# Two projection units fewer ahead of the first gather, and six units beside the first V products

## The chip, the cores and the metric

The kernel runs on one core of a Trainium2 chip. The metric is the device time of the whole program in microseconds (us). The program drives five engines: TensorE (PE in the profile; PEld is its weight load), VectorE (DVE), ScalarE (ACT), GpSimd (POOL), which here issues the gathers, and SyncE (SP), which issues all other DMAs. The engines run their own instruction streams in program order and meet at semaphores.

## The reference

One layer of a streaming encoder in float32. It is run on a prompt of 1024 rows and on a sample of 32 rows, with the same weights:

```python
h = rmsnorm(x, norm_mix_w);  proj = h @ w_in            # 1024 x 2824
# proj: mLSTM q, k, v, output gate, input and forget gates | attention q, k, v
hm = sigmoid(mo) * head_rmsnorm(mlstm_scan(mq, mk, mv, gates))   # 4 heads of 128
hs = swa(rope(sq), rope(sk), sv, sinks)                          # 8 heads, window 128
x = x + concat(hm, hs) @ w_out
h2 = rmsnorm(x, norm_ffn_w)
# PEER: per row and each of 8 heads, the best 16 of 128 x 128 experts
s1, s2 = keys of both halves of (h2 @ w_q);  idx = best 16 sums of two keys
a = gelu(peer_u[idx] . h2);  x = x + sum(softmax(top) * a * peer_v[idx])
y = rmsnorm(x, norm_final_w)
```

## The kernel before

The rows are cut into nine tiles: tiles 0 to 7 are 128 rows of the prompt, the last is the sample. A tile is projected (`h @ w_in`, in six chunks of 512 columns, the last of 264), mixed (mLSTM and attention, output projection, second norm, queries, key scores), and then goes through the expert stage.

**Expert stage.** A tile's 128 rows go in groups: 32 rows by four heads fill the 128 partitions, and two groups `g` belong to 32 rows. Each group has 16 steps. One step, called a slot `t = 16 g + k`, gathers 128 rows of `peer_u` (for the next group) and 128 rows of `peer_v` (for this group), 0.524 MB each. POOL issues them in turn, U then V, in one queue (`gather_u`, `gather_v`). DVE multiplies U rows by the normalised rows and sums (L1261, a dot); ACT takes the gelu; DVE makes the weights `wk`; PE multiplies them by V rows and adds up in the PSUM tensor `acc` (L1657, a V product). U rows land in a ring of six buffers, V rows in one of seven; a gather waits until its buffer is free. There are 66 groups, 1056 slots, 2112 gathers. The first 16 U gathers, those of group 0, stand at slots -16 to -1.

**Order of the work.** For every engine it is written out. After tile 0, the steps of each later tile's mixing are hung on slots: `slot_of(m, r)` gives the slot of a step with rank `r` of tile `m`; PE_AT, ACT_AT and DVE_AT hold the ranks. On PE rank 5 transposes q and k (`qk_transpose`), 11 to 25 are the mLSTM, 33 to 54 the attention, 58 to 65 the output projection, 75 to 90 the 16 `query` steps, 91 to 94 the key scores. At its slot a step follows the V product on PE and the dot on DVE.

**Before the first gather.** Tile 0 has nothing else to hide behind, so its mixing up to the concatenation is interleaved with other work: projections of tiles 1 to 3, in units. A unit is one chunk of columns for one tile, `(c, m)` in UNITS, and has two halves of four matmuls. There are 18 units for tiles 1 to 3. BEHIND of them are interleaved with tile 0's mixing in `first_tiles`; EARLY_AT says after which half unit which ranks of tile 0 stand. One unit more (number BEHIND) is put between tile 0's output projection and its second transposes. The rest stand on PE at the slots in UNIT_PE, their copies out of PSUM at those in UNIT_ACT (even units) and UNIT_DVE (odd units). All 18 use two halves of `acc` in turn, which is also what V products add into, so the first V product waits until all units are copied (`begin_parts(0)`).

A unit is copied to a buffer (UNIT_PO names it), and SP stores it from there to a scratch tensor in DRAM; tile `m`'s mixing loads it from there (`load_p`). Buffers 5 to 9 are the last three V buffers of the ring, so `gather_v` of the slots 4, 5 and 6 waits until all units that use these buffers are stored. SP also loads the query weights `w_q` in four pieces of 2 MB (`load_wq`) to the place of input weights that no unit needs any more: the first takes the place of chunk 2, the other three those of chunks 3 to 5.

Of the kernel before, what the change touches and what calls it, by code (L numbers as in the profile page):

```python
# [15 lines left out]
DC = D // P  # L16
# [77 lines left out]
EARLY_AT = ((10, 0), (14, 2), (20, 4), (24, 6), (32, 7), (36, 9), (46, 11), (50, 14), (54, 15), (EARLY_END, 16))  # L94


UNITS = [(c, m) for c in range(3) for m in range(1, FIRST)]
BEHIND = len(UNITS)
UNITS += [(3, 1), (4, 1), (5, 1), (3, 2), (3, 3), (4, 2), (4, 3), (5, 2), (5, 3)]
UNIT_PE = {-16: 10, -14: 11, -12: 12, -10: 13, -8: 14, -6: 15, -4: 16, -2: 17}  # L100
UNIT_ACT = {-12: 10, -7: 12, 1: 14, 3: 16}
UNIT_DVE = {-11: 11, -4: 13, 1: 15, 4: 17}

UNIT_PO = [(0, 1, 2, 3, 4, 8)[n % 6] for n in range(BEHIND)] + [4, 5, 6, 7, 8, 9, 4, 5, 6]
# [12 lines left out]
def slot_of(m, r):  # L117

    if m == 1:
        return -4 + r * 85 // 100  # L120
    if m == 2:
        return 78 + r * 120 // 100
    if m == 3:
        return 206 + r * 85 // 100 if r < 51 else 264 + (r - 51) * 88 // 100
    base = AGAIN + PERIOD * NC_ + 1 if m == FIRST else 8 * TOPK * (m - 1)
    points = {FIRST: SLOTS_4, FIRST + 1: SLOTS_5, SAMPLE: SLOTS_SAMPLE}.get(m, SLOTS)
    for (r0, s0), (r1, s1) in zip(points, points[1:]):
        if r <= r1:
            return base + s0 + (r - r0) * (s1 - s0) // (r1 - r0)
# [46 lines left out]
def program(nc, x_prompt, x_sample, cache_k, cache_v, st_c, st_n, st_m, norm_mix_w, w_in, if_bias, mnorm_w, sinks,  # L176
# [15 lines left out]
    with ExitStack() as ctx:  # L192
# [99 lines left out]
        po += [part[:, :]] + [ring[:, NU + 4, 0:512]] + [a[:, h * 512:h * 512 + 512] for a in (ring[:, NU + 5, :], ring[:, NU + 6, :]) for h in range(2)]  # L292
        first = [pj[:, 0:512], pj[:, 512:1024], vx[:, :, 0:MD], pj[:, 1024:1536], pj[:, 1536:2048], pj[:, 2048:PJ]]
# [8 lines left out]
        unit_bank = [acc[:, 0:512], acc[:, 512:1024]]  # L302
# [11 lines left out]
        proj_out = [sem(f"proj_out{b}") for b in range(10)]  # L314
# [43 lines left out]
        def _(sp):  # L358
# [134 lines left out]
            sp.wait_ge(chunk_ready, NC_ + 9)  # L493
            load_wq(0)

# [27 lines left out]
            for b in range(10):  # L523
                sp.wait_ge(proj_out[b], stored(b, len(UNITS)))
# [81 lines left out]
        def _(act):  # L606
# [64 lines left out]
            def unit_copy(n):  # L671
# [5 lines left out]
                S.activation(po[b][:, 0:PC[c][1]], unit_bank[n % 2][:, 0:PC[c][1]], ACT.Copy, scale=nr1[:, m, 2:3])  # L677
# [27 lines left out]
            def mix(s, i, m):  # L705
# [197 lines left out]
        def _(dve):  # L903
# [34 lines left out]
            def unit_copy(n):  # L938
# [4 lines left out]
                V.tensor_scalar(po[b][:, 0:PC[c][1]], unit_bank[n % 2][:, 0:PC[c][1]], nr1[:, m, 2:3], None, ALU.mult)  # L943
# [41 lines left out]
            def mix(s, i, m):  # L985
# [13 lines left out]
                elif s == "qk_copy":  # L999
# [6 lines left out]
                    dve.wait_ge(qk_transposed, m + 1)  # L1006
                    V.tensor_scalar(qkT[:, 4:8, 0:n], mx[:, 3, :].rearrange("p (h t) -> p h t", h=4)[:, :, 0:n], MD ** -0.5, None, ALU.mult)
# [290 lines left out]
        def _(pe):  # L1298
# [315 lines left out]
            def begin_parts(q):  # L1614
# [103 lines left out]
```

## Time and profile before

| | |
|---|---|
| median of 3 runs | 3126.98 us (3126.38 to 3129.21) |
| the profiled execution, its span | 3386.3 us |
| PE busy | 2600.2 us (77%) |
| DVE busy | 2120.6 us (63%) |
| POOL busy | 1995.2 us (59%) |
| ACT busy | 556.3 us (16%) |
| mean DMA rate | 353 GB/s |
| mean granted TensorE clock | 0.811 |

The profiled execution is longer than the timed ones. Its span starts with the first instruction and ends with the last. In a row of the timeline stand the start, the time from start to end, the engine, the line, the operation, what it writes and reads, how many instructions were merged (a float32 matmul is two), and in brackets the idle time of the engine before it and what ended that. "DMA" in the windows is the mean busy share of the 16 DMA engines, "PEclk" the granted TensorE clock as a share of full speed.

### The profile page before, as it was taken

To read this page: it belongs to the slowest core of one execution; us is meant where nothing else is said; L and a number is where in the kernel's file an instruction comes from. 1 tells how busy PE (TensorE), PEld (TensorE's weight loads), DVE (VectorE), ACT (ScalarE), POOL (GpSimd) and SP (SyncE) were. 2 spreads that over 40 slices of the span, in tenths; PEclk is the share of its full clock that TensorE was granted. 3 is DMA by queue.
4 is the path that set the end of the run, shared out by engine and by line. 5 is a ranking of instruction groups with operands and counts; after the bars stand their busy time and mean duration, and the time that the engine had idled before them with its cause. 6 is when DMAs were issued, how large, how long until landed. Compare 5 with 4: busy or idle time off the path is not lost.

```text
span 3386.3 us, 33673 instructions
## 1 busy us (share of the span) xinstructions
PE 2600.2 (77%) x10989; PEld 1007.2 (30%) x10989; DVE 2120.6 (63%) x5282; ACT 556.3 (16%) x1093; POOL 1995.2 (59%) x2128
## 2 busy tenths in 40 slices
PE   8996886678678899987876876678676776686666
PEld 4562351225222533223432331124212331121101
DVE  1256657766676666657667757676667666676653
ACT  2211111211121131122012111111111011111001
POOL 0026556666666566665656666666666666666665
PEclk9997897789677899997987887788667886677667
DMA  6479999999999999999999999999999999999998
GB/s 230 146 275 371 336 338 374 362 371 343 378 351 365 342 400 407 409 382 353 362 329 346 380 354 381 367 364 345 384 360 360 370 365 376 358 368 370 371 363 332
DMA packets 348919, 1197.02 MB, mean 353 GB/s; under 512 B 37760, under 2 KB 54408, under 8 KB 346952
## 3 DMA queue, kind: packets, MB, share of 16 engines
q0 software_dynamic: 304128, 1107.43, 86.7%
q1 hardware_dynamic: 44616, 87.45, 7.0%
q8 instruction: 86, 1.41, 0.2%
q14 instruction: 89, 0.73, 0.1%
HBM read 1180.69 MB, written 14.15 MB: 353 GB/s over the span
## 4 chain that ended last, share of the span: by engine, by line
PE 33%; DVE 16%; issue 13%; POOL 12%; DMA 9%; another core or an unknown queue 8%; DVEq 6%; ACT 1%; ACTq 0%; SPq 0%; POOLq 0%
PE acc L1657 11%; PE mx L1549 7%; DVE ring L1261 7%; POOL ring L593 6%; POOL ring L582 6%; DMA ring<-in_peer_v_dram,idx 5%; DVEq L1148 4%; DMA ring<-in_peer_u_dram,idx 4%; PE mx L1365 3%; PE mx L1531 2%; PE acc L1341 2%; PE mx L1560 2%; PE acc L1328 1%; PE h2p L1603 1%
## 5 line engine op out<-in xcount | busy, mean ns | idle before, releaser
L1657 PE MATMUL acc<-ring,wk 128*32 128x512 f32 x4224 | 1362.6, 742 | 525.6 <-DMA ring<-in_peer_v_dram,idx 289.4
L1261 DVE SCALAR_TENSOR_TENSOR ring<-ring,h2p 128x1024 f32<-128x1024 f32 x1056 | 1273.8, 1215 | 565.4 <-DMA ring<-in_peer_u_dram,idx 315.8
L593 POOL DMA_INDIRECT ring<-in_peer_v_dram,idx x1056 | 997.1, 944 | 707.7 <-issue 269.7
L582 POOL DMA_INDIRECT ring<-in_peer_u_dram,idx x1056 | 996.3, 943 | 667.1 <-issue 292.9
L1657 PEld LDWEIGHTS acc<-ring,wk 128*32 128x32 f32 x4224 | 217.8, 122 | 1406.6 <-issue 670.8
L1549 PE MATMUL mx<-reg,weights 128*128 128x128 f32 x1792 | 256.7, 297 | 40.9 <-issue 38.6
L1549 PEld LDWEIGHTS mx<-reg,weights 128*128 128x128 f32 x1792 | 230.8, 206 | 145.7 <-issue 145.7
L1531 PE MATMUL mx<-weights,reg 128*128 128x512 f32 (+1 forms) x256 | 133.0, 643 | 3.5 <-issue 3.5
L1365 PE MATMUL mx<-weights 128*128 128x512 f32 (+1 forms) x288 | 126.9, 585 | 0.0
L821 ACT ACTIVATE gl<-dots 128x16 f32<-128x16 f32 x66 | 14.2, 216 | 637.5 <-issue 346.1
L1603 PE MATMUL h2p<-ch,ident 32*32 32x512 f32 x528 | 86.7, 708 | 36.6 <-issue 18.9
L1560 PE MATMUL mx<-kT,pj 128*32 128x128 f32 x1040 | 69.4, 313 | 32.9 <-issue 25.3
L781 ACT COPY pj<-mx 128x512 f32<-128x512 f32 x32 | 18.7, 585 | 432.0 <-remote 182.7
L1261 DVE DVE_READ_ACCUMULATOR ring<-ring,h2p 128x1 f32 x1056 | 86.9, 82 | 0.0
L821 ACT ACT_TABLE_LOAD x66 | 84.7, 1283 | 6.5 <-issue 1.1
L815 ACT ACT_TABLE_LOAD x61 | 78.3, 1283 | 19.1 <-issue 11.3
L1365 PEld LDWEIGHTS mx<-weights 128*128 128x128 f32 x288 | 53.4, 195 | 75.8 <-issue 74.3
L1531 PEld LDWEIGHTS mx<-weights,reg 128*128 128x128 f32 (+1 forms) x256 | 44.1, 189 | 96.4 <-issue 96.4
L1560 PEld LDWEIGHTS mx<-kT,pj 128*32 128x32 f32 x1040 | 50.1, 123 | 64.6 <-issue 54.8
L1224 DVE TENSOR_TENSOR xt<-xt,acc 32x1024 f32<-32x1024 f32 x33 | 40.1, 1216 | 45.0 <-PE acc L1612 32.2
L1087 DVE TENSOR_REDUCE s<-mx 128x4 f32<-128x1024 f32 (+1 forms) x18 | 21.0, 1174 | 58.9 <-remote 46.6
L1365 PE MATMUL mx<-weights,reg 128*128 128x512 f32 (+1 forms) x96 | 47.4, 642 | 12.4 <-DMA weights<-in_w_in_dram 6.6
(310 smaller groups left out, 2400.3 us busy)
## 6 DMA issues: line engine op xcount, KB each, us to landing
ring<-in_peer_u_dram,idx POOLq DMA_INDIRECT x1056
ring<-in_peer_v_dram,idx POOLq DMA_INDIRECT x1056
weights<-in_peer_w_q_dram SPq DMA_DIRECT2D x7, 2048.0 KB
weights<-in_w_in_dram SPq DMA_DIRECT2D x5, 2048.0 KB, 18.2
weights<-in_w_in_dram SPq DMA_DIRECT2D x10, 1024.0 KB
ring<-in_peer_w_q_dram SPq DMA_DIRECT2D x8, 1024.0 KB, 5.6
xt<-in_x_prompt_dram SPq DMA_DIRECT2D x8, 512.0 KB
ring<-in_w_out_dram SPq DMA_DIRECT2D x2, 2048.0 KB, 14.2
```

What stands on the lines that cost most here:

```text
L582: pool.indirect_dma_start(ring[:, n % NU, :], None, u_d, bass.IndirectOffsetOnAxis(ap=idx[:, g % 4, k:k + 1], axis=0)).then_inc(u_in[n % N ...
L593: pool.indirect_dma_start(ring[:, NU + n % NV, :], None, v_d, bass.IndirectOffsetOnAxis(ap=idx[:, g % 4, k:k + 1], axis=0)).then_inc(v_in[ ...
L815: S.activation(ew[:, :], top[:, g % 3, :], ACT.Exp, bias=ntop[:, g % 3:g % 3 + 1], accum_out=ez[:, 0:1])
L821: S.activation(gl[:, :], dots[:, g % 2, :], ACT.Gelu)
L1148: dve.drain()
L1261: V.scalar_tensor_tensor(ring[:, n % NU, :], ring[:, n % NU, :], 1.0, h2p[:, :], ALU.mult, ALU.mult, accum_out=dots[:, (g + 1) % 2, k:k + ...
L1365: last = T.matmul(bank, hT1_again[i][:, 4 * half + k, :], wpiece[(2 * p + half) % 3][:, k, 0:w], start=half + k == 0, stop=half == 1 and k ...
L1531: last = T.matmul(mx[0:n, 2 + half, :], t8[:, k, 0:n], w, start=k == 0, stop=k == DC - 1)
L1549: last = T.matmul(mx[:, i // 4, i % 4 * P:i % 4 * P + n], w, t8[:, k, 0:n], start=k == 0, stop=k == DC - 1)
L1560: last = T.matmul(mx[q:q + SUB, i, col:col + NK], qT[:, c, i * SUB:(i + 1) * SUB], kT[:, c % 2, :], start=True, stop=True)
L1603: last = T.matmul(h2p[j * SUB:(j + 1) * SUB, cols], ident[r, r], ch[m % 2][r, cols], start=True, stop=True)
L1657: last = T.matmul(acc[j:j + SUB, cols], wk[:, g % 2, n % TOPK, :], ring[:, NU + n % NV, cols], start=g % 2 == 0 and n % TOPK == 0, stop=g ...
```

## The change

UNITS is cut otherwise: ahead of the first gather now stand seven units and not nine in the interleaved part (both chunks 0 and 1 of the three tiles, and chunk 2 of tile 1), and then one after the output projection as before. Chunk 2 of tiles 2 and 3 goes behind the first gather. EARLY_AT spreads tile 0's steps over 14 half units and not 18.

Of the ten units behind the first gather, four (8 to 11) stand at slots -16 to -7, ahead of the V products. Six (12 to 17, from LATE on) stand at slots 1 to 13 and write to the banks 0 and 1 of the PSUM tensor `mx`, which is otherwise the mixing's. They are copied to four new buffers, 10 to 13, in the SBUF tensor `reg`, also the mixing's. V products wait for the copies of units 0 to 11 only, and slots 4 to 6 of the V gathers for units 8 to 11. Tile 1's mixing begins at slot 16 and not -4 and takes 61 slots per 100 ranks and not 85; it waits for the late units' copies and stores. The first piece of `w_q`, which takes chunk 2's place, is loaded behind unit 11.

```diff
-EARLY_AT = ((10, 0), (14, 2), (20, 4), (24, 6), (32, 7), (36, 9), (46, 11), (50, 14), (54, 15), (EARLY_END, 16))
-UNITS = [(c, m) for c in range(3) for m in range(1, FIRST)]
+EARLY_AT = ((10, 0), (14, 2), (20, 3), (24, 5), (32, 6), (36, 8), (46, 9), (50, 11), (54, 12), (EARLY_END, 13))
+UNITS = [(c, m) for c in range(2) for m in range(1, FIRST)] + [(2, 1)]
 BEHIND = len(UNITS)
-UNITS += [(3, 1), (4, 1), (5, 1), (3, 2), (3, 3), (4, 2), (4, 3), (5, 2), (5, 3)]
-UNIT_PE = {-16: 10, -14: 11, -12: 12, -10: 13, -8: 14, -6: 15, -4: 16, -2: 17}
+UNITS += [(3, 1), (4, 1), (5, 1), (2, 2), (2, 3), (3, 2), (3, 3), (4, 2), (4, 3), (5, 2), (5, 3)]
+LATE = 12
+UNIT_PE = {-16: 8, -13: 9, -10: 10, -7: 11, 1: 12, 3: 13, 6: 14, 8: 15, 11: 16, 13: 17}
...
-UNIT_PO = [(0, 1, 2, 3, 4, 8)[n % 6] for n in range(BEHIND)] + [4, 5, 6, 7, 8, 9, 4, 5, 6]
+UNIT_PO = [(0, 1, 2, 3, 4, 8)[n % 6] for n in range(BEHIND)] + [4, 5, 6, 7, 8] + [10, 11, 12, 13, 10, 11]
...
     if m == 1:
-        return -4 + r * 85 // 100
+        return 16 + r * 61 // 100
...
+        po += [reg[:, 512 * i:512 * i + 512] for i in range(4)]
...
-        unit_bank = [acc[:, 0:512], acc[:, 512:1024]]
+        unit_bank = [acc[:, n % 2 * 512:n % 2 * 512 + 512] if n < LATE else mx[:, n % 2, :] for n in range(len(UNITS))]
...
             for n in range(6, BEHIND):
                 store_unit(n)
-            sp.wait_ge(chunk_ready, NC_ + 9)
-            load_wq(0)
...
                     act.wait_ge(qk_transposed, m + 1)
+                    if m == 1:
+                        for b in range(10, 14):
+                            act.wait_ge(proj_out[b], stored(b, len(UNITS)))
...
                         pe.wait_ge(chunk_dve if n % 2 else chunk_act, 3 + n // 2)
+                        if n == LATE:
+                            pe.wait_ge(sc_ready, 1)
...
+                    elif m == 1:
+                        pe.wait_ge(chunk_act, 3 * FIRST)
+                        pe.wait_ge(chunk_dve, 3 * FIRST)
+                        pe.wait_ge(p_in, p_landed(m))
+                        pe.wait_ge(sc_ready, m)
...
                 elif q == 0:
-                    pe.wait_ge(chunk_act, 3 * FIRST)
-                    pe.wait_ge(chunk_dve, 3 * FIRST)
+                    pe.wait_ge(chunk_act, 3 + LATE // 2)
+                    pe.wait_ge(chunk_dve, 3 + LATE // 2)
```

PE at the first V products, in the kernel before. `mx<-kT,pj` are tile 0's last key scores, `acc<-weights` with `ch1` or `xt1` are units of tiles 2 and 3, `acc<-ring,wk` are V products (two matmuls each), `mx<-ident,pj` is tile 1's first mixing step.

```order
L1560 MATMUL mx<-kT,pj 32x128 x56
L1341 MATMUL acc<-weights 128x512 x8
L1341 MATMUL acc<-weights 128x264 x8
L1341 MATMUL acc<-weights,ch1 128x512 x8
L1341 MATMUL acc<-weights,xt1 128x512 x8
L1341 MATMUL acc<-weights,ch1 128x512 x8
L1341 MATMUL acc<-weights,xt1 128x512 x8
L1341 MATMUL acc<-weights,ch1 128x264 x8
L1341 MATMUL acc<-weights,xt1 128x264 x8
L1436 MATMUL mx<-ident,pj 128x128 x8
L1657 MATMUL acc<-ring,wk 32x512 x12
```

The same place in the changed kernel, where L1348 are units and L1669 V products.

```order
L1572 MATMUL mx<-kT,pj 32x128 x56
L1348 MATMUL acc<-weights 128x512 x8
L1348 MATMUL acc<-weights 128x264 x8
L1348 MATMUL acc<-weights,ch1 128x512 x8
L1348 MATMUL acc<-weights,xt1 128x512 x8
L1348 MATMUL mx<-weights,ch1 128x512 x8
L1669 MATMUL acc<-ring,wk 32x512 x6
L1348 MATMUL mx<-weights,xt1 128x512 x8
L1669 MATMUL acc<-ring,wk 32x512 x6
L1348 MATMUL mx<-weights,ch1 128x512 x8
L1669 MATMUL acc<-ring,wk 32x512 x4
L1348 MATMUL mx<-weights,xt1 128x512 x8
```

Five units stand ahead of the first V product in place of eight, then units and V products alternate.

PE in the query steps of tile 1, in the kernel before. L1549 is one `query` step (eight matmuls), L1657 a V product.

```order
L1549 MATMUL mx<-reg,weights 128x128 x8
L1657 MATMUL acc<-ring,wk 32x512 x2
L1549 MATMUL mx<-reg,weights 128x128 x8
L1657 MATMUL acc<-ring,wk 32x512 x2
L1549 MATMUL mx<-reg,weights 128x128 x8
L1657 MATMUL acc<-ring,wk 32x512 x2
L1549 MATMUL mx<-reg,weights 128x128 x16
```

The same place in the changed kernel.

```order
L1561 MATMUL mx<-reg,weights 128x128 x8
L1669 MATMUL acc<-ring,wk 32x512 x2
L1561 MATMUL mx<-reg,weights 128x128 x16
L1669 MATMUL acc<-ring,wk 32x512 x2
L1561 MATMUL mx<-reg,weights 128x128 x8
L1669 MATMUL acc<-ring,wk 32x512 x2
L1561 MATMUL mx<-reg,weights 128x128 x16
```

From the first to the last of the 16 query steps there were 13 V products, now there are 9.

## Rows read from the trace of the kernel before

**Rows 1.** Window of 20 us ahead of the first gather: span, busy time by engine, PEclk, DMA, GB/s.

```profile
60.00:80.00 20.00, 20.00 (x80) 11.14 (x79) 3.35 (x15) 4.30 (x11) 0.00 (x0) 1.00 0.08 28
```

**Rows 2.** Timeline of POOL: U gathers L582, V gathers L593, from the first on.

```profile
191.99 1.09 POOL L582 DMA_INDIRECT ring<-in_peer_u_dram,idx  x1 [189.34 <-DVEq L1204]
...
230.84 0.94 POOL L593 DMA_INDIRECT ring<-in_peer_v_dram,idx  x1 [0.30 <-issue]
...
259.67 0.94 POOL L593 DMA_INDIRECT ring<-in_peer_v_dram,idx  x1 [19.19 <-DMA proj_scratch<-ring]
...
264.84 0.94 POOL L593 DMA_INDIRECT ring<-in_peer_v_dram,idx  x1 [3.00 <-DMA proj_scratch<-ring]
```

**Rows 3.** Windows of the gather stage, columns as in rows 1 (the number of POOL's gathers in brackets).

```profile
250.00:255.00 5.00, 1.43 (x11) 1.07 (x9) 2.73 (x9) 2.75 (x5) 0.00 (x0) 1.00 1.02 424
255.00:260.00 5.00, 0.00 (x0) 0.00 (x0) 1.59 (x3) 0.00 (x0) 0.33 (x1) 0.53 0.47 187
260.00:265.00 5.00, 3.85 (x10) 1.06 (x12) 3.66 (x11) 0.00 (x0) 1.70 (x3) 0.50 0.75 237
305.00:477.00 172.00, 139.10 (x561) 60.40 (x561) 120.02 (x300) 28.19 (x62) 104.27 (x111) 0.81 0.93 344
3200.00:3300.00 100.00, 64.54 (x158) 7.29 (x158) 56.49 (x119) 6.94 (x11) 66.70 (x71) 0.62 0.97 366
```

**Rows 4.** Timeline of PE, tile 0's mixing with half units (L1341, eight instructions each).

```profile
110.47 2.96 PE L1490 MATMUL mx<-ktw,reg 64*128 64x256 f32 x16
113.36 7.13 PE L1341 MATMUL acc<-weights 128*128 128x512 f32 x16
120.33 3.60 PE L1341 MATMUL acc<-weights,ch 128*128 128x512 f32 x8
123.76 0.27 PE L1496 MATMUL mx<-ident,reg 128*128 128x128 f32 x1
...
135.95 1.04 PE L1513 MATMUL mx<-ident,ch 128*128 128x128 f32 x8
136.83 3.60 PE L1341 MATMUL acc<-weights,xt 128*128 128x512 f32 x8
```

**Rows 5.** Timeline of ACT and DVE in that stretch: the softmax's last step, the copy of the concatenation.

```profile
120.06 0.25 ACT L753 ACTIVATE s<-s 128x8 f32<-128x8 f32 x1
...
137.03 0.69 DVE L1121 TENSOR_TENSOR reg<-mx,mnw 128x512 f32<-128x512 f32 x1 [3.23 <-PE mx L1513]
```

**Rows 6.** Timeline of PE and DVE from the first gather on: units, weights `wk`, first V products.

```profile
205.27 10.69 PE L1341 MATMUL acc<-weights 128*128 128x512 f32 x32
215.80 7.03 PE L1341 MATMUL acc<-weights,ch 128*128 128x512 f32 x16
...
229.21 1.22 DVE L1261 SCALAR_TENSOR_TENSOR ring<-ring,h2p 128x1024 f32<-128x1024 f32 x1
...
238.43 0.69 DVE L1216 TENSOR_TENSOR wk<-rept,coef 128x512 f32<-128x512 f32 x1
...
261.15 6.63 PE L1657 MATMUL acc<-ring,wk 128*32 128x512 f32 x20 [9.73 <-DVEq L944]
```

**Rows 7.** DMA issues by line: KB each, median us to landing.

```profile
weights<-in_peer_w_q_dram SPq DMA_DIRECT2D x7, 2048.0 KB
proj_scratch<-ring SPq DMA_DIRECT2D x5, 256.0 KB, 11.5
```

**Rows 8.** Timeline of PE in tile 1's query steps (L1549, 16 instructions each).

```profile
457.89 2.05 PE L1549 MATMUL mx<-reg,weights 128*128 128x128 f32 x16
459.88 1.05 PE L1657 MATMUL acc<-ring,wk 128*32 128x512 f32 x4
460.86 3.84 PE L1549 MATMUL mx<-reg,weights 128*128 128x128 f32 x32
464.63 1.05 PE L1657 MATMUL acc<-ring,wk 128*32 128x512 f32 x4
```

**Rows 9.** What POOL waited for from 460 to 500 us: us in total, times, longest.

```profile
POOL ring L593 <- PE acc L1657: 10.2, 7, 2.6
```

More of the change, by code:

```diff
@@ L93 @@
 SLOTS = ((0, -56), (50, 2), (57, 11), (58, 13), (65, 20), (66, 22), (74, 30), (75, 32), (91, 57), (95, 62))
-EARLY_AT = ((10, 0), (14, 2), (20, 4), (24, 6), (32, 7), (36, 9), (46, 11), (50, 14), (54, 15), (EARLY_END, 16))
-UNITS = [(c, m) for c in range(3) for m in range(1, FIRST)]
+EARLY_AT = ((10, 0), (14, 2), (20, 3), (24, 5), (32, 6), (36, 8), (46, 9), (50, 11), (54, 12), (EARLY_END, 13))
+UNITS = [(c, m) for c in range(2) for m in range(1, FIRST)] + [(2, 1)]
 BEHIND = len(UNITS)
-UNITS += [(3, 1), (4, 1), (5, 1), (3, 2), (3, 3), (4, 2), (4, 3), (5, 2), (5, 3)]
-UNIT_PE = {-16: 10, -14: 11, -12: 12, -10: 13, -8: 14, -6: 15, -4: 16, -2: 17}
-UNIT_ACT = {-12: 10, -7: 12, 1: 14, 3: 16}
-UNIT_DVE = {-11: 11, -4: 13, 1: 15, 4: 17}
-UNIT_PO = [(0, 1, 2, 3, 4, 8)[n % 6] for n in range(BEHIND)] + [4, 5, 6, 7, 8, 9, 4, 5, 6]
+UNITS += [(3, 1), (4, 1), (5, 1), (2, 2), (2, 3), (3, 2), (3, 3), (4, 2), (4, 3), (5, 2), (5, 3)]
+LATE = 12
+UNIT_PE = {-16: 8, -13: 9, -10: 10, -7: 11, 1: 12, 3: 13, 6: 14, 8: 15, 11: 16, 13: 17}
+UNIT_ACT = {-14: 8, -8: 10, 3: 12, 8: 14, 13: 16}
+UNIT_DVE = {-11: 9, -5: 11, 5: 13, 10: 15, 15: 17}
+UNIT_PO = [(0, 1, 2, 3, 4, 8)[n % 6] for n in range(BEHIND)] + [4, 5, 6, 7, 8] + [10, 11, 12, 13, 10, 11]
 def rows_of(m):
@@ L313, in program @@
         chunk_act, chunk_dve = sem("chunk_act"), sem("chunk_dve")
-        proj_out = [sem(f"proj_out{b}") for b in range(10)]
+        proj_out = [sem(f"proj_out{b}") for b in range(14)]
         wout_in, wq_in = sem("wout_in"), sem("wq_in")
@@ L522, in _ @@
             load_x(1)
-            for b in range(10):
+            for b in range(14):
                 sp.wait_ge(proj_out[b], stored(b, len(UNITS)))
@@ L676, in unit_copy @@
                     act.wait_ge(proj_out[b], stored(b, n))
-                S.activation(po[b][:, 0:PC[c][1]], unit_bank[n % 2][:, 0:PC[c][1]], ACT.Copy, scale=nr1[:, m, 2:3])
+                S.activation(po[b][:, 0:PC[c][1]], unit_bank[n][:, 0:PC[c][1]], ACT.Copy, scale=nr1[:, m, 2:3])
                 act.drain().then_inc(chunk_act, 1)
@@ L942, in unit_copy @@
                     dve.wait_ge(proj_out[b], stored(b, n))
-                V.tensor_scalar(po[b][:, 0:PC[c][1]], unit_bank[n % 2][:, 0:PC[c][1]], nr1[:, m, 2:3], None, ALU.mult)
+                V.tensor_scalar(po[b][:, 0:PC[c][1]], unit_bank[n][:, 0:PC[c][1]], nr1[:, m, 2:3], None, ALU.mult)
                 dve.drain().then_inc(chunk_dve, 1)
@@ L1006, in mix @@
                     dve.wait_ge(qk_transposed, m + 1)
+                    if m == 1:
+                        for b in range(10, 14):
+                            dve.wait_ge(proj_out[b], stored(b, len(UNITS)))
                     V.tensor_scalar(qkT[:, 4:8, 0:n], mx[:, 3, :].rearrange("p (h t) -> p h t", h=4)[:, :, 0:n], MD ** -0.5, None, ALU.mult)
@@ L1340, in project_unit @@
                     for k in range(4 * half, 4 * half + 4):
-                        last = T.matmul(unit_bank[n % 2][:, 0:PC[c][1]], hT1[m][:, k, :], win_s[c][:, k, :], start=k == 0, stop=k == DC - 1)
+                        last = T.matmul(unit_bank[n][:, 0:PC[c][1]], hT1[m][:, k, :], win_s[c][:, k, :], start=k == 0, stop=k == DC - 1)
                     if half == 1:
```

## The prediction

> **What bounds the kernel now.** I read the windows first, then POOL's timeline, then PE's, and the waits last. The program has two parts, and the first gather, issued at 191.99 us [rows 2], divides them. I call that moment S and give times after it as S+...
>
> Ahead of S the DMA engines are nearly idle and PE is busy without a gap at full clock: 20.00 of 20 us at a DMA share of 0.08 [rows 1]. Tile 0's chain of mixing runs through PE, half units fill the places where it would wait, and the reader should see that one instruction follows the other. So an instruction less on PE there is time less, as long as what it covered is not late itself.
>
> Behind S the transfers bound it. 2112 gathers and the other loads go through the same engines. Between 305 and 477 us, while tile 1 is mixed, POOL issues 111 gathers in 172 us, 3.10 us per slot of two; in the last tile, with hardly any mixing, 71 in 100 us, 2.82 us per slot [rows 3]. The DMA share is 0.93 and 0.97, so mixing costs some tenths of a microsecond per slot, and the rest is transfer.
>
> The join of the parts is where the change works. POOL reaches the V gather of slot 4 at 240.5 us and stands there 19.19 us, until 259.67, for a unit's store; the gather of slot 5 goes at 264.84, S+72.9, after another 3.00 us of waiting for a store [rows 2]. The backlog of transfers lasts until 255 us (424 GB/s from 250 to 255), and then there is a hole: 187 and 237 GB/s in the two next slices of 5 us [rows 3]. PE has the same story: `wk` is ready at 239.1 us (238.43 plus 0.69), S+47, but the first V product starts at 261.15, S+69, behind a unit's copy [rows 6].
>
> **The change part by part.** The sum is made in the profiled execution, whose span of 3386.3 us is 8.3% above the median of 3126.98 us. Terms ahead of S are engine times. Those behind S could be some 8% smaller in a timed run, at most half a microsecond on each, so I take them over as they are.
>
> *The lead.* Four half units leave the stretch ahead of S: one between gate sums and running maximum, one before and one after the attention scores, one after the concatenation. A half unit takes 3.43 us from its start to the next instruction's (120.33 to 123.76) [rows 4], so four take 13.7 us. What did they cover? After the scores, the softmax needs from 113.43 us (110.47 plus 2.96) to 120.31 (120.06 plus 0.25), 6.9 us [rows 4, 5]; two half units stay there and take 7.0 us (113.36 to 120.33), so about 0.2 us may show. After the concatenation nothing stays: the copy ends at 137.72 (137.03 plus 0.69) [rows 5], and PE, which went on at 136.83 [rows 4], will go on at about 138.0, 1.1 us later. At the other two places the half unit that stays covers what is left. The lead is 13.7 - 0.2 - 1.1 = 12.4 us, between 10 (each of the four places shows a microsecond) and 13.7. The first load of `w_q` disappears ahead of S too; it hid beside PE and gives nothing there.
>
> *The hole.* A unit takes 7.0 us on PE, one of 264 columns 3.7 (10.69 for one of each, less 7.03), and units ran from S+13.3 (205.27) without a gap [rows 6]. Units 8 to 11 are three of the one and one of the other, 24.7 us. So unit 11 is through at about S+38. Its copy on DVE stands behind the dot at slot -5, which ended at 230.4 (229.21 plus 1.22), S+38.5 [rows 6], so SP stores it at S+39.5. POOL's first V gather is at 230.84, S+38.8 [rows 2]; at 1.24 us per gather (0.94 of work and 0.30 between) its turn comes to slot 5 at S+51 and to slot 6, the last that waits for a store, at S+53.7. A store to the scratch that meets the gathers lands 11.5 us after its issue [rows 7], that is S+51. So POOL no longer stops, by a margin of under 3 us. What this is worth depends on whether the transfers or POOL bound the stretch. If transfers, only the hole closes: 237 and 187 GB/s missing over 5 us each [rows 3] are 2.1 MB, and at 424 GB/s 5.0 us. If POOL, slot 5 goes at S+51.2 in place of S+72.9: 21.7 us. With no gain at all as the other end, I take 5.0, because 424 GB/s were moved up to 255 us while POOL issued nothing: the backlog was real.
>
> *Bytes moved behind S.* One piece of `w_q`, 2.10 MB [rows 7], and the stores of two units, 0.52 MB, ran in the idle time ahead of S and now run among the gathers: 2.62 MB. At 424 GB/s [rows 3] that is 6.2 us; at 344, the rate while tile 1 is mixed, 7.6 us; nothing, if they fall into gaps. I take 6.2, as they go into the full stretch behind S+40. For this the Trainium skill ("DMA: Bandwidth & Descriptors", Specifications) gives a limit of about 358 GB/s for one core's share of the memory. The slice at 424 GB/s does not agree with it; by that limit the term would be 7.3 us and the sum 1.1 us worse.
>
> *Six units beside V products.* They take 35 us of PE (four times 7.0 and twice 3.7) between V products of slots 1 to 13. The first V product can go at about S+49, when `wk` and the second V row are there, 20 us earlier than before; up to slot 13 PE then needs 35 us for units and 14 for products and is there at about S+98, while the transfers bring V rows no faster than before. The ring of seven covers the rest, so this costs nothing; if that cover failed, V gathers would stop for PE, and one unit of 7.0 us is the bound. Their bank waits are for copies on ACT and DVE several slots earlier. Behind PE's new wait at tile 1's first step V products queue, but the last copy is at slot 15 and the step at slot 19. The late units' stores must be through at slot 20, five slots or 14 us after the copy, longer than the 11.5 us [rows 7]. On SP the first piece of `w_q` now stands behind unit 11's store and ahead of unit 12's; its issue holds nothing up, and nobody needs `w_q` before tile 1's queries at slot 61. Tile 1's rows are loaded after the stores of units 7 to 9, as before after three stores, long before slot 19.
>
> *Tile 1 squeezed.* Its mixing had 80 slots and has 58. A query step takes 1.98 us and a V product 0.98 on PE (457.89, 459.88, 460.86, 464.63) [rows 8]. Before, 16 steps stood among 13 products: 44.4 us of PE. Now they stand among 9: 40.5 us, and the four slots fall elsewhere at 2.82 us or more [rows 3], 11.3 us: 7.4 us longer. The output projection likewise has two products fewer, 3.7 us. That is 11.1 us if no ring slack takes it up, and nothing if it takes up all. V gathers already waited 10.2 us for PE at these steps before [rows 9], so some will show; but a stage at 2.97 us per slot was near the pace, and the ring holds seven V rows, some 20 us, when the steps begin. I take 4 us.
>
> The sum: -12.4 - 5.0 + 6.2 + 4.0 = -7.2 us. The profiled span would go to 3379.1, the median to 3119.8 us, and S to 179.6 us.
>
> **The rivals.** *POOL bounds the start (3097 us).* If transfers have room, the whole 21.7 us count and the moved bytes cost nothing: -12.4 - 21.7 + 4 = -30.1. For it: the timed runs are 8% faster than the profiled one, so the backlog may drain sooner there. Against it: the 424 GB/s without any issue.
>
> *Tile 1's mixing holds the gathers up (3134 us).* The place is slots 16 to 74, where 88 ranks stand that used to lie partly at the join, where V products stood still anyway. At the pace of before, mixing cost 0.28 us per slot (3.10 - 2.82) over 56 slots and 67 ranks, 15.7 us; 88 ranks would cost 4.9 us more. With the 11.1 us of queries and projection that is 16.0, and if waits grow as the steps crowd, up to 24. It is slower than before from 11.2 us on (12.4 + 5.0 - 6.2), and measurably so from 17.5; at 18 it gives +6.8. For it: V gathers already wait for PE there. Against it: PE was busy only 139 of 172 us [rows 3], and a lag shorter than the ring costs nothing.
>
> *The hole moves and does not close (3125 us).* A late store of unit 11, or V products behind units, stops POOL again a few slots on: -12.4 + 6.2 + 4 = -2.2. The margin of under 3 us at slots 5 and 6 speaks for it. For a late store the Trainium skill ("DMA: Bandwidth & Descriptors", Queues, rings and completion order) has a cause: an engine serves the queues that have work in turn, so a store shares with the gathers; the 11.5 us [rows 7] agree, and by it the store would be in time only just.
>
> **How the numbers follow.** A measurement of this kernel can tell about 0.2%, 6.3 us, from no change. The forecast has a chance of 0.50, with a range of its own from 3112 to 3126; its middle lies just beyond the 6.3 us, so 0.33 of it counts as faster, 0.15 as the same and 0.02 as slower. POOL's rival has 0.15, all faster. The hole that moves has 0.19: 0.02, 0.16 and 0.01. The squeezed tile has 0.16: 0.02 the same and 0.14 slower. Together: faster 0.50, same 0.33, slower 0.17. The range runs from 3102 to 3132; it leaves out the far halves of the first two rivals.
>
> **What would show it.** The lead: the first U gather at 179 to 182 us. The hole: no wait of POOL for a store, V products from S+50, slices of 5 us at over 400 GB/s from S+45 to S+85. The bytes: gather of slot 20 some 11 us earlier than before, not 30. The squeeze: POOL's waits for V products in tile 1's query steps, more than 10 us in 40. From tile 2 on both kernels should have the same pace. I am wrong if the first gather does not come 10 us earlier, if the gain at slot 20 is over 20 us, or if tile 1 gives more than 11 us back.

## The result and the profile after

The changed kernel is slower: 3132.73 us (median of 12 runs, 3130.89 to 3136.86) against 3127.38 us for the kernel before on the same chip, ratio 1.0021 with a 95% interval from 1.0013 to 1.0029. That is +6.6 us, from +4.1 to +9.1. The forecast was 3119.8 us, and slower had a chance of 0.17.

The profiled execution that [rows 1 to 9] come from had a span of 3386.3 us and ran slower than the timed runs. So the profile after (span 3135.1 us) is compared with a second profile of the kernel before, span 3125.1 us, which is the first experiment below. Its first gather stands at 191.81 us, against 191.99 in [rows 2].

POOL's timeline in the kernel after: start, time from start to end, line (L581 gathers U, L592 gathers V), and in brackets the idle time before and what ended it.

```profile
184.38 1.09 POOL L581 DMA_INDIRECT ring<-in_peer_u_dram,idx  x1 [181.72 <-DVEq L1209]
...
219.21 0.94 POOL L592 DMA_INDIRECT ring<-in_peer_v_dram,idx  x1 [0.30 <-issue]
...
229.15 0.94 POOL L592 DMA_INDIRECT ring<-in_peer_v_dram,idx  x1 [0.31 <-issue]
...
249.65 0.93 POOL L592 DMA_INDIRECT ring<-in_peer_v_dram,idx  x1 [5.56 <-PE acc L1669]
...
268.31 0.94 POOL L592 DMA_INDIRECT ring<-in_peer_v_dram,idx  x1 [4.19 <-PE acc L1669]
```

The first gather comes 7.4 us earlier, not 12.4. The V gather of slot 4, the fifth of V, goes at 229.15, with no stop since the first one at 219.21; the 19.19 us of [rows 2] (19.72 in the second profile) are gone. In their place stand shorter waits for V products that stand behind a late unit (5.56 and 4.19 us above).

What the earlier start and the closed hole are worth is read from the bytes, by kind, in the same two stretches of both kernels: 184 to 281 us and 281 to 356 us. q0 is the gathers' queue. After:

```profile
DMA packets 9881, 35.05 MB, mean 361 GB/s; under 512 B 1127, under 2 KB 1794, under 8 KB 9108
q0 software_dynamic: 6922, 25.24, 69.4%
...
DMA packets 8340, 30.80 MB, mean 411 GB/s; under 512 B 917, under 2 KB 1146, under 8 KB 8079
q0 software_dynamic: 7657, 27.88, 93.1%
```

The kernel before, second profile:

```profile
DMA packets 8498, 29.77 MB, mean 307 GB/s; under 512 B 984, under 2 KB 1893, under 8 KB 7723
q0 software_dynamic: 5398, 19.69, 55.4%
...
DMA packets 8419, 30.69 MB, mean 409 GB/s; under 512 B 935, under 2 KB 935, under 8 KB 8415
q0 software_dynamic: 8415, 30.64, 102.5%
```

From 184 to 356 us the kernel after has moved 65.85 MB against 60.46, 5.39 MB more, which at 410 GB/s are 13.1 us. Of these, 7.4 are the lead. The other 5.7 are what is left for the hole, which can be read by itself too: the kernel before moved 279 and 133 GB/s in the 5 us from 250 and from 255 us on, 2.0 MB short of 410 GB/s, or 5.0 us. But of the 5.39 MB only 2.79 are gathers (53.12 against 50.33). The other 2.60 MB are the loads and stores that the change moved behind the first gather: 6.3 us. So the gathers are 6.8 us ahead. The second stretch shows it in the open: both kernels move 410 GB/s there, but before all of it is gathers, and after 2.9 MB of it are not.

Then the gain is lost. The windows from the V gather of slot 20 to that of slot 44, and on to that of slot 80, by the times at which POOL issues them, first after, then before (columns as in [rows 1]; the last three are the clock, the DMA share and GB/s):

```profile
280.74:355.69 74.95, 51.11 (x200) 16.02 (x199) 56.97 (x160) 18.17 (x38) 45.56 (x48) 0.84 1.03 411
355.69:477.56 121.87, 106.72 (x672) 61.69 (x673) 78.40 (x184) 18.10 (x40) 67.70 (x73) 0.89 0.88 317
```

```profile
298.93:359.65 60.72, 44.25 (x185) 14.77 (x178) 52.33 (x142) 16.73 (x42) 45.10 (x48) 0.89 1.03 409
359.65:468.70 109.05, 97.24 (x503) 50.55 (x504) 75.66 (x178) 13.19 (x21) 68.11 (x72) 0.91 0.97 366
```

At slot 20 the kernel after is 18.2 us ahead, as 280.74 against 298.93 show. But that is a head start of gathers over other transfers, which catch up by slot 44: there it is 4.0 us ahead, with the engines at 411 and 409 GB/s in both. From slot 44 to slot 80 it needs 121.87 us where the kernel before needs 109.05: 12.8 us lost, at 317 GB/s against 366 and a DMA share of 0.88 against 0.97. At slot 80 it is 8.9 us behind, at slot 100 9.3, at slot 1055 10.1. From tile 2 on little happens any more. In the changed kernel the slots from 44 to 80 hold the end of tile 1's attention, its output projection, residual, queries and key scores.

### The profile page after: what moved, and what is told of

It is laid out like the page before. It is cut to its first block, busy times and chain, and to the rows that moved or that the text cites. A ratio compares the mean times of both kernels' runs of the same rounds, so it can differ in the third digit from the quotient of the medians.

```text
span 3135.1 us, 33679 instructions
## 1 busy us (share of the span) xinstructions
PE 2512.6 (80%) x10989; PEld 954.7 (30%) x10989; DVE 2133.0 (68%) x5282; ACT 556.1 (18%) x1093; POOL 1996.1 (64%) x2128
## 4 chain that ended last, share of the span: by engine, by line
DMA 35%; PE 34%; DVE 11%; POOL 10%; issue 5%; DVEq 4%; ACT 1%; SPq 0%; ACTq 0%; POOLq 0%
DMA ring<-in_peer_u_dram,idx 20%; DMA ring<-in_peer_v_dram,idx 13%; PE acc L1669 10%; PE mx L1561 6%; POOL ring L592 5%; POOL ring L581 5%; DVE ring L1266 5%; PE mx L1543 4%; PE mx L1372 2%; DVEq L1153 2%; PE acc L1348 2%; PE acc L1333 1%; PE h2p L1615 1%; DMA weights<-in_w_in_dram 1%; PE mx L1499 1%
## 5 line engine op out<-in xcount | busy, mean ns | idle before, releaser
L1669 PE MATMUL acc<-ring,wk 128*32 128x512 f32 x4224 | 1332.5, 733 | 535.2 <-DMA ring<-in_peer_v_dram,idx 462.9
L1266 DVE SCALAR_TENSOR_TENSOR ring<-ring,h2p 128x1024 f32<-128x1024 f32 x1056 | 1279.6, 1217 | 565.5 <-DMA ring<-in_peer_u_dram,idx 507.3
L581 POOL DMA_INDIRECT ring<-in_peer_u_dram,idx x1056 | 1000.2, 947 | 695.5 <-DVE ring L1266 236.8
L592 POOL DMA_INDIRECT ring<-in_peer_v_dram,idx x1056 | 994.1, 941 | 426.1 <-issue 260.6
L1669 PEld LDWEIGHTS acc<-ring,wk 128*32 128x32 f32 x4224 | 194.1, 120 | 1423.0 <-DMA ring<-in_peer_v_dram,idx 1003.3
L1561 PEld LDWEIGHTS mx<-reg,weights 128*128 128x128 f32 x1792 | 213.6, 196 | 92.3 <-issue 92.3
L1561 PE MATMUL mx<-reg,weights 128*128 128x128 f32 x1792 | 233.5, 286 | 0.0
L1543 PE MATMUL mx<-weights,reg 128*128 128x512 f32 (+1 forms) x256 | 130.1, 635 | 0.3
L1615 PE MATMUL h2p<-ch,ident 32*32 32x512 f32 x528 | 75.6, 693 | 15.6 <-DVEq L1269 15.6
L1266 DVE DVE_READ_ACCUMULATOR ring<-ring,h2p 128x1 f32 x1056 | 87.2, 83 | 0.0
L1543 PEld LDWEIGHTS mx<-weights,reg 128*128 128x128 f32 (+1 forms) x256 | 43.3, 186 | 88.2 <-issue 84.5
L753 ACT ACTIVATE reg<-mx,s 128x256 f32<-128x256 f32 (+1 forms) x72 | 32.3, 471 | 99.8 <-DVEq L1099 99.8
L1221 DVE TENSOR_TENSOR wk<-rept,coef 128x512 f32<-128x512 f32 x66 | 45.9, 695 | 5.9 <-issue 0.8
L1572 PE MATMUL mx<-kT,pj 128*32 128x128 f32 x1040 | 44.1, 279 | 0.7 <-ACTq L784 0.7
L1624 PE MATMUL acc<-part,ident 32*32 32x512 f32 x66 | 44.1, 754 | 0.7 <-ACTq L835 0.7
## 6 DMA issues: line engine op xcount, KB each, us to landing
weights<-in_peer_w_q_dram SPq DMA_DIRECT2D x7, 2048.0 KB, 13.9
ring<-in_w_out_dram SPq DMA_DIRECT2D x2, 2048.0 KB, 14.1
```

What stands on the lines that cost most here:

```text
L581: pool.indirect_dma_start(ring[:, n % NU, :], None, u_d, bass.IndirectOffsetOnAxis(ap=idx[:, g % 4, k:k + 1], axis=0)).then_inc(u_in[n % N ...
L592: pool.indirect_dma_start(ring[:, NU + n % NV, :], None, v_d, bass.IndirectOffsetOnAxis(ap=idx[:, g % 4, k:k + 1], axis=0)).then_inc(v_in[ ...
L1266: V.scalar_tensor_tensor(ring[:, n % NU, :], ring[:, n % NU, :], 1.0, h2p[:, :], ALU.mult, ALU.mult, accum_out=dots[:, (g + 1) % 2, k:k + ...
L1543: last = T.matmul(mx[0:n, 2 + half, :], t8[:, k, 0:n], w, start=k == 0, stop=k == DC - 1)
L1561: last = T.matmul(mx[:, i // 4, i % 4 * P:i % 4 * P + n], w, t8[:, k, 0:n], start=k == 0, stop=k == DC - 1)
L1615: last = T.matmul(h2p[j * SUB:(j + 1) * SUB, cols], ident[r, r], ch[m % 2][r, cols], start=True, stop=True)
```

## The experiments

Times are medians, ratios are to the kernel before on the same chip with their 95% interval.

**The kernel before once more.** No edit; its profile is used above.

> The kernel before, unchanged, looked at once more, because its profiled execution (span 3386.3 us) was 8% above its median and the one of the changed kernel (span 3135.1 us) is not. Theory A (the changed kernel loses in tile 1's squeezed mixing): a span near 3130 us, first gather at 190 to 192 us, V gather of slot 20 about 10 us later than the changed kernel's 280.7 us, that of slot 80 less than 2 us later or already earlier than its 477.6 us. Theory B (it loses at the late units beside V products): slot 20 already within 3 us of 280.7 us, slot 80 likewise.

3126.86 us, span 3125.1. Slot 80 comes earlier than the changed kernel's, as theory A said, but slot 20 is 18.2 us later and not 10.

**The squeeze alone.**

```diff
     if m == 1:
-        return -4 + r * 85 // 100
+        return 16 + r * 61 // 100
```

> The kernel before, with tile 1's mixing alone moved to slots 16 to 74 (16 + r*61/100). Theory A, the squeeze costs the 11 to 18 us: 3138 to 3145 us. Theory B, the late units beside V products or the moved bytes cost it: 3125 to 3131 us.

3143.06 us against 3128.95, ratio 1.0046 [1.0032, 1.0059]: +14.1 us. Tile 1's new slots alone cost more than the whole change, and in the profile 12.3 us are lost between slots 44 and 80. The forecast had this term at 4, with 11.1 as its upper bound.

**Late units and squeeze, nine units ahead as before.**

```diff
+LATE = 12
+UNIT_PE = {-16: 10, -13: 11, 1: 12, 3: 13, 6: 14, 8: 15, 11: 16, 13: 17}
...
+        return 16 + r * 61 // 100
```

> Nine units ahead of the first gather as before, with the first piece of w_q ahead too, but the last six units beside V products and tile 1's mixing squeezed as in the changed kernel. Theory A (squeeze): the hole at the join closes, 5 us, and the squeeze takes 11 to 18: 3133 to 3140 us, as much as the squeeze alone or a little less. Theory B (late units cost): more than the squeeze alone by 5 us or over. If the hole is worth what was forecast and the squeeze 4 us: 3126 us.

3138.72 us, ratio 1.0031 [1.0019, 1.0043]: +9.8 us. Beside the squeeze the late units bring some 4 us, about what the closed hole is worth, though the two intervals overlap.

**The lead alone: seven units ahead, the other ten in front of the V products in `acc`, tile 1's old slots.**

```diff
+EARLY_AT = ((10, 0), (14, 2), (20, 3), (24, 5), (32, 6), (36, 8), (46, 9), (50, 11), (54, 12), (EARLY_END, 13))
...
+UNIT_PE = {-16: 8, -14: 9, -13: 10, -12: 11, -10: 12, -9: 13, -8: 14, -6: 15, -4: 16, -2: 17}
```

> Seven units ahead as in the changed kernel, the first piece of w_q behind the first gather, but all ten others ahead of the V products in acc, and tile 1's mixing at its old slots. The lead of 7.6 us (184.38 against 191.99 us in the two profiles) against 6.2 us of moved bytes and about 7 us by which V products start later after the first gather. Theory A: 3128 to 3135 us, no better than before. If moved bytes cost nothing: 3120 us.

3120.78 us, ratio 0.9974 [0.9962, 0.9986]: -8.2 us. The lead is real and stays, but its first gather is at 184.25 us like the changed kernel's: 7.6 us, not 12.4. The expectation that moved bytes and later V products would eat this lead failed; the time is the one that it named for moved bytes that cost nothing. Its profile leaves that open: it moved 51.67 MB of gathers up to 356 us against 50.33, only 3.3 us ahead, and gained 5.8 us more between slots 44 and 80.

**Tile 1's queries and scores alone.**

```diff
-        return -4 + r * 85 // 100
+        return -4 + r * 85 // 100 if r < 75 else 62 + (r - 75) * 61 // 100
```

> The kernel before, with only tile 1's ranks from 75 on (query steps and key scores) packed, to slots 62 to 74. Theory Q (PE in the query steps holds the gathers up, the place the forecast named): 5 to 9 us above before. Theory D (DVE stands at the residual until PE's packed output projection is through, its dots stop, and the U ring fills): within 2 us of before, since the projection stays at its old density.

3129.18 us against 3128.25, ratio 1.0004 [0.9995, 1.0013]: nothing. The query steps, on which the forecast put two thirds of its bound (7.4 of 11.1 us), are not the place.

**The ranks below 58 alone (mLSTM, attention, concatenation).**

```diff
-        return -4 + r * 85 // 100
+        return 16 + r * 50 // 100 if r < 58 else -4 + r * 85 // 100
```

> The kernel before, with only tile 1's ranks below 58 (mLSTM, attention, concatenation) packed, to slots 16 to 44, denser than in the changed kernel; projection, residual, norm, queries and scores at their old slots. Theory D: within 3 us of before. Theory C (all ranks crowd each other, each costs its wait): 6 us or more above before. Theory Q: as before.

3133.69 us, ratio 1.0022 [1.0012, 1.0032]: +5.4 us by the medians, between theory D and theory C. Part of the loss is the front's, here packed more densely than in the changed kernel. VectorE's wait at the residual stays at 6.7 us, and the loss stands elsewhere: from slot 20 to 44 the profile needs 69.61 us in place of 60.72, from 44 to 80 only 103.97 in place of 109.05.

**The changed kernel with these slots**, so with the ranks from 58 on at their old places.

```diff
-        return 16 + r * 61 // 100
+        return 16 + r * 50 // 100 if r < 58 else -4 + r * 85 // 100
```

> The changed kernel with tile 1's ranks below 58 at slots 16 to 44 and all others at the slots of the kernel before. Theory D: the 11 to 14 us of the squeeze come back, 3118 to 3122 us. Theories C and Q: 3128 to 3133 us, little better than the changed kernel.

3124.89 us, ratio 0.9987 [0.9978, 0.9996]. Against the changed kernel's 1.0021 these are 10.6 us, give or take 3.8; the time lies between theory D's range and that of the others. Their first gathers agree (184.45 and 184.38). Between slots 44 and 80 this kernel takes 107.72 us, the changed one 121.87, and VectorE's wait at the residual is 6.70 us. The loss sits in the ranks from 58 on, as they stand behind a squeezed front.

What happens there shows in the kernel after on two engines. PE first (L1531 are the transposes of the norm's weights, L1543 the output projection):

```profile
391.71 3.75 PE L1531 MATMUL mx<-ffw,ident 8*128 8x128 f32 x16 [3.97 <-DVEq L1128]
...
397.24 5.26 PE L1543 MATMUL mx<-weights,reg 128*128 128x512 f32 x8
...
413.82 3.70 PE L1543 MATMUL mx<-weights,reg 128*128 128x512 f32 x8
```

VectorE in the same stretch (L1136 is the residual, L1198 work of the top-k of one of tile 0's later groups, L1266 dots), and then POOL's next gather of U:

```profile
402.30 0.43 DVE L1198 TENSOR_TENSOR cand<-cand,i2f 128x256 f32<-128x256 f32 x1
417.56 1.22 DVE L1136 TENSOR_TENSOR xt<-xt,mx 128x1024 f32<-128x1024 f32 x1 [14.83 <-PE mx L1543]
418.90 1.22 DVE L1266 SCALAR_TENSOR_TENSOR ring<-ring,h2p 128x1024 f32<-128x1024 f32 x1
...
420.40 0.94 POOL L581 DMA_INDIRECT ring<-in_peer_u_dram,idx  x1 [5.29 <-DVE ring L1266]
```

PE stands 3.97 us for VectorE's copy of the concatenation and begins the projection late; its first eight instructions take 5.26 us, where later ones take 3.70; the granted clock is 0.52 from 390 to 395 us and 0.50 from 395 to 400. It ends at 417.5. VectorE has reached the residual at 402.7 and stands there for 14.83 us. It runs in order, so no dot is computed meanwhile, no U buffer comes free, and POOL stands for 5.29 us. In the kernel before the same wait was 6.69 us:

```profile
403.30 1.22 DVE L1131 TENSOR_TENSOR xt<-xt,mx 128x1024 f32<-128x1024 f32 x1 [6.69 <-PE mx L1531]
```

What POOL waited for from 320 to 480 us (us in total, times, longest), after and before:

```profile
POOL ring L592 <- PE acc L1669: 23.2, 14, 4.0
POOL ring L581 <- DVE ring L1266: 15.7, 10, 5.3
...
POOL ring L581 <- DVEq L1209: 5.2, 3, 2.3
```

```profile
POOL ring L593 <- PE acc L1657: 16.5, 20, 2.6
...
POOL ring L582 <- DVE ring L1261: 9.8, 11, 3.6
POOL ring L582 <- DVEq L1204: 2.1, 2, 1.5
```

44.1 us against 28.4; both rings give more, V for PE 6.7 and U for VectorE 9.0. Two experiments test whether VectorE's stand is the price.

**The output projection packed, in the kernel before.**

```diff
-        return -4 + r * 85 // 100
+        return 50 + (r - 58) * 50 // 100 if 58 <= r < 75 else -4 + r * 85 // 100
```

> The kernel before, with one edit: tile 1's ranks 58 to 74 (output projection, residual, second norm, second transposes) stand in slots 50 to 58 and not in 45 to 58; all other ranks keep their slots. Theory D (VectorE runs in order and stands at the residual until TensorE's packed output projection is through; no dots meanwhile, so the U ring fills): VectorE's wait at the residual grows from 6.7 to 12 us or more, and the time rises by 6 to 9 us, about the 8.7 by which the squeeze of all ranks is dearer than that of the ranks below 58. Rival P (every slot taken from tile 1 costs the same, wherever it is): 5 of the 22 slots go, 14.1 x 5 / 22 = +3.2 us.

3125.51 us against 3127.66, ratio 0.9993 [0.9984, 1.0002]. Neither came: no loss of 6 to 9 us, and not the 3.2 of the rival either. The trace says why the first did not: the wait that was to grow to 12 us grew to 8.78 only.

```profile
408.99 1.22 DVE L1131 TENSOR_TENSOR xt<-xt,mx 128x1024 f32<-128x1024 f32 x1 [8.78 <-PE mx L1531]
```

PE began this projection at 391.41 without a stand ahead of it. So packing the projection was harmless where PE came to it in time. My first form of the theory falls: the packing alone does not make VectorE stand. That PE's lateness does is read from the rows above, not tested by itself.

**The residual three slots later, in the changed kernel.**

```diff
-        return 16 + r * 61 // 100
+        return 16 + r * 61 // 100 + (3 if r >= 66 else 0)
```

> The kernel after, with one edit: tile 1's ranks from 66 on (residual, second norm, second transposes, queries, key scores) stand three slots later, 59 to 76; the output projection keeps its slots 51 to 55. Theory D: VectorE finds the projection done, its wait at the residual falls from 14.8 us to under 7, and the kernel is 4 to 7 us faster than the kernel after: 3126 to 3129 us. Rival P (the packing as such, TensorE's work per slot): nothing or 1 us, since the projection and the queries are packed as densely as before: 3132 us.

3126.62 us, ratio 0.9998 [0.9987, 1.0009]: against the changed kernel's 1.0021, 7.2 us faster, give or take 4.3. PE's stand ahead of the transposes is the same, 3.98 us, and the projection packed as before; VectorE's wait is 8.04, a little over the 7 expected. Its row:

```profile
412.17 1.22 DVE L1136 TENSOR_TENSOR xt<-xt,mx 128x1024 f32<-128x1024 f32 x1 [8.04 <-PE mx L1543]
```

The windows from 400 to 440 us, here and then in the changed kernel:

```profile
400.00:420.00 20.00, 20.00 (x73) 6.47 (x72) 10.85 (x18) 4.01 (x5) 11.25 (x13) 1.00 0.86 293
420.00:440.00 20.00, 16.39 (x114) 11.52 (x113) 16.68 (x46) 1.97 (x4) 15.12 (x17) 1.00 1.01 396
```

```profile
400.00:420.00 20.00, 20.00 (x58) 6.42 (x58) 4.81 (x9) 1.15 (x2) 6.55 (x7) 0.99 0.78 271
420.00:440.00 20.00, 15.82 (x90) 9.61 (x87) 18.35 (x48) 4.24 (x6) 13.90 (x15) 0.83 0.86 299
```

VectorE is busy 10.85 us in place of 4.81, POOL issues 13 gathers and not 7, and the next 20 us run at 396 GB/s in place of 299. As these are the same times but not the same slots (the residual comes 5.4 us earlier here), the stretch between slots 44 and 80 says it better:

```profile
352.94:461.84 108.90, 94.32 (x510) 51.76 (x509) 79.55 (x185) 17.53 (x39) 67.92 (x72) 0.94 0.95 359
```

The changed kernel took 121.87 us there and the kernel before 109.05: the loss of this stretch is gone. The other profiles agree. In the four with a wait of 12.27 to 14.91 us at the residual (the changed kernel, the squeeze alone, late units with squeeze, and the changed kernel with other places, below) the stretch takes 117.97 to 121.87 us; in the nine with 6.69 to 8.78 it takes 103.24 to 109.76. The wait falls on both rings: POOL's waits of the stretch go from 37.6 to 21.2 us, for V products from 23.2 to 13.9. Over the whole program 7.2 us come back, about half of the squeeze's 14, and even these need not all be VectorE's stand: the profile's first gather came at 179.88 us, 4.5 before the changed kernel's, by another course of the clock (see below). From slot 80 to 100 it loses 2.8 us again. The queries moved three slots on with the residual here; that these cost little was shown above only for their packing.

**The half units of the lead at other places.** The lead alone with two half units between gate sums and running maximum, none between the attention's transposes and its scores, one after the concatenation:

```diff
+EARLY_AT = ((10, 0), (14, 2), (20, 4), (24, 5), (32, 6), (36, 8), (46, 8), (50, 10), (54, 11), (EARLY_END, 12))
```

> The lead alone (seven units ahead, ten others ahead of the V products, old slots for tile 1), with the same 14 half units at other places: two between gate sums and running maximum, none between attention transposes and scores, one behind the concatenation. Theory K (the lead lost 5 us to TensorE's clock, granted at 0.66 from 75 to 80 us and at 0.6 to 0.75 from 130 to 140, behind stretches of small matmuls or a wait): first gather at 180 to 182 us in place of 184.25, clock 1.00 in these slices, and 3116 to 3119 us. If the clock falls elsewhere or the new wait at the scores costs as much: 184 us and 3120 us.

3117.18 us, ratio 0.9962 [0.9949, 0.9975]: -11.1 us, better than both kernels. Its first gather is at 179.06, 12.8 us before that of the kernel before, near the forecast's 12.4, though with other places. Of the 5.2 us between this and the lead alone, the granted clock accounts for most. Two steps of PE in the changed kernel, whose first gather agrees with the lead alone's (two half units; tile 0's output projection):

```profile
76.09 8.83 PE L1348 MATMUL acc<-weights,xt 128*128 128x512 f32 x16
...
131.78 16.87 PE L1543 MATMUL mx<-ring,reg 128*128 128x512 f32 x32
```

Windows there, with the granted clock as the third column from the right:

```profile
75.00:80.00 5.00, 5.00 (x17) 2.76 (x16) 1.84 (x6) 1.35 (x5) 0.00 (x0) 0.66 0.14 48
...
130.00:135.00 5.00, 5.00 (x17) 3.06 (x16) 0.00 (x0) 0.00 (x0) 0.00 (x0) 0.58 0.00 0
135.00:140.00 5.00, 5.00 (x10) 2.06 (x9) 0.00 (x0) 0.00 (x0) 0.00 (x0) 0.74 0.00 0
```

The projection and the windows in the kernel with the other places:

```profile
129.33 14.00 PE L1528 MATMUL mx<-ring,reg 128*128 128x512 f32 x32
```

```profile
75.00:80.00 5.00, 5.00 (x26) 3.22 (x25) 0.45 (x4) 0.67 (x3) 0.00 (x0) 1.00 0.06 23
...
130.00:135.00 5.00, 5.00 (x13) 2.14 (x12) 0.00 (x0) 0.00 (x0) 0.00 (x0) 1.00 0.05 18
135.00:140.00 5.00, 5.00 (x13) 2.28 (x12) 0.00 (x0) 0.00 (x0) 0.00 (x0) 1.00 0.45 129
```

Two half units take 8.83 us where two took 7.13 in [rows 4], the projection 16.87 where it takes 14.00: 4.6 us together. At 0.58 to 0.74 of full speed a part of each slice ran at 1.2 GHz. It fell behind stretches of small products: 18 instructions on 4 partitions (L1469 to L1472) ahead of 76, and ahead of 130 the transposes on 8 partitions with a stand of 0.90 us before them. The same stretches do not always bring it: in the kernel with the later residual, which has the same order up to there, the half units stay at full speed and the projection takes 15.70 us.

```profile
74.92 7.13 PE L1348 MATMUL acc<-weights,xt 128*128 128x512 f32 x16
```

**The same places in the changed kernel**, and **in the changed kernel with the old slots from rank 58 on**:

> The kernel after, with the half units ahead of the first gather at other places (two between gate sums and running maximum, none between the transposes of the attention and its scores, one after the concatenation). Theory (the clock's dips cost the lead 5 us): granted clock 1.00 in 70 to 85 and 125 to 140 us, first gather at 179 us and not 184, and 4 to 5 us faster than the kernel after: 3128 us, no difference from the kernel before. Rival (tile 1's mixing, which stands by slots, gives an earlier start back again): first gather at 179, but the time stays at 3131 to 3133 us.

> The kernel after with both repairs: the half units ahead of the first gather at the other places, and of tile 1 only the ranks below 58 moved (16 + r x 50 / 100), the rest at the slots of before. If the two repairs add, 3.4 + 4.5 = 8 us faster than the kernel before: 3119 us. If the earlier start is given back in the squeezed front of tile 1: 3124 us, no better than with the second repair alone. With all ten units ahead of the V products the same places gave 11.1 us, so the late units and the squeeze that they need would still cost about 3 us.

3131.33 us, ratio 1.0014 [1.0005, 1.0023], and 3122.45 us, ratio 0.9983 [0.9974, 0.9992]. Against their counterparts with the diff's places these are 2.2 and 1.3 us faster, with the lead alone 3.8; each with 4 to 6 us of uncertainty, so a gain of 4 to 5 us is not confirmed. The first time lies where its rival put it (tile 1 gives the earlier start back), the second between its two expectations. The profiles show why it can be less: the dips come and go between kernels with one order. With the diff's places the first gather stood at 184.38, 184.25, 184.45 and 179.88 us (the last in the kernel with the later residual), with the others at 179.06, 179.18 and 181.0, where one dip was left: means of 183.2 and 179.7. With nine units ahead the clock stood at 1.00 in every slice from 60 to 180 us in five profiles of six; the sixth, of the packed projection, fell to 0.69 from 80 to 85 us, and its first gather came at 194.69. That the places, or the number of units, decide is likely from these thirteen profiles, not shown.

## Why the prediction was wrong, step by step

**The squeezed tile (+4, bounds 0 and 11.1) failed.** It costs 14.1 us alone, and 12.8 us are lost in the changed kernel from slot 44 to 80. Two things were wrong in the step. The price was worked out on PE alone, as instructions per slot, with the ring of V rows as its cover. The costly wait is VectorE's for PE at the residual, 14.83 us in place of 6.69, and with it the U ring runs out too, which the step did not look at: of the 15.7 us by which POOL's waits grew, 9.0 are on U. And the place was wrong: queries +0.9, the projection -2.2, each packed alone and with an interval that holds zero; together they had been the whole 11.1. The front, for which the main sum had nothing, costs 5.4 when squeezed alone, and behind it PE comes late to what follows. The second rival, "tile 1's mixing holds the gathers up", had the right outcome, 3134 us, mostly on the wrong steps: 11.1 of its 16 us were queries and projection. Its other 4.9, for the crowding as such, are near the 5.4 of the front. Its evidence against, that PE was busy for only 139 of 172 us [rows 3], was beside the point: a late engine need not be a busy one.

**The lead (-12.4) came to -7.4** in the two profiles compared; by the means of all profiles with these orders (192.7 us in six, 183.2 in four) it is -9.4. What failed is that the durations of the half units, and of the projection behind them, were taken at full clock: the dips account for 4.6 of the 5.0 us that are missing. Its counting is borne out by the other places, where the clock stayed at 1.00 and the first gather came 12.8 us earlier. The step's own end was -10.

**The hole (-5.0) was right:** POOL waits for no store, every slice of 5 us from 229 to 269 us runs at 407 GB/s or more, and by the bytes it is worth 5.0 to 5.7 us. V products begin at 228.30, S+43.9, earlier than the S+50 expected. The rival with 21.7 us fell: the transfers bound the stretch. At slot 20 the gain of 18.2 us looked like it, and only the bytes by queue tell that 2.60 MB of it were put off.

**The moved bytes (+6.2) were right as bytes:** 2.60 MB by the queues against 2.62, 6.3 us at 410 GB/s. That they lengthen the program by as much is not shown: the lead alone moves the same loads and stores and is still 8.2 us faster, as much as its whole lead. The limit of about 358 GB/s that the Trainium skill gives ("DMA: Bandwidth & Descriptors", Specifications) does not hold here, as 75 us at 411 GB/s show.

**The late units (0) were nearly right.** POOL waits behind them for V products, 5.56 and 4.19 us at the longest, but the engines moved 408 GB/s in the slice from 245 to 250 us, in which POOL issued one gather: the backlog covers it.

Together: -7.4 - 5.7 + 6.3 + 12.8 = +6.0, against +6.6 measured. That these come so near is in part luck, as the sum mixes two measures. The first three are bytes, by which the kernel after is 6.8 us ahead at 356 us; the 12.8 lie between times of issue, by which it is only 4.0 ahead at slot 44. By times of issue alone it is 8.9 behind at slot 80, and the two profiled spans differ by 10.0 us: the profiled execution of the kernel after is the longest of its twelve. Of the tests, two said "wrong" and both were met: the first gather not 10 us earlier, and tile 1 giving more than 11 us back. The test on query steps was a bad one: POOL waits 14.3 us for V products from 440 to 480 us after, but the kernel before has 11.3 us from 430 to 470 as well.

**Not settled:** why the front alone costs 5 us; whether the places of the half units decide the clock's dips; what the moved bytes cost in the end; and why the lead alone (-8.2) and late units with squeeze (+9.8) add to +1.6 and not to +6.6 (5 us apart, with an uncertainty of about 6). The late units on top of the best version cost rather than pay: 3122.45 (ratio 0.9983) with them and a squeezed front, 3117.18 (0.9962) without either.

## What to carry to other kernels

Before steps are packed closer, go through every place where one engine's in-order stream waits for another's, and ask what stands behind the waiting instruction and which ring that empties; the load of the busiest engine doesn't tell it. A gain at a join is read in bytes of the transfers that bound it, by queue, well behind the join, since an early lead of one kind of transfer may only be other transfers put off. Where filling work is taken from between small products, read the granted clock again there: here the dips cost 4.6 of the 12.4 us that were to be freed.

## What the runs showed of the hardware beyond that

- With work waiting, the DMA engines settle at one rate: from 300 to 340 us 409 or 410 GB/s at a share of 1.03 in all thirteen profiles used here, and over 75 us 411 in the kernel after and 409 in the one before.
- The same order of PE instructions ahead of the first gather gave first gathers from 179.88 to 184.45 us in four profiles, by how far the granted clock dipped behind small products; with nine units ahead six profiles had 191.81 to 194.69, that at 194.69 with a dip.
